# Recurrent layers of a hybrid encoder: three buffers for the mixed inputs, projections in another order, mixing in two groups, and two modulation rounds moved

## What is computed

```python
shift, scale, gate = split(silu(c) @ W_mod + b_mod)
hn = rmsnorm(x) * (1 + scale) + shift
x = x + gate * mixer(hn)
```

```python
xx = 0.5 * (shift_right(h) + shift_left(h)) - h
mu_cols = concat(mu[i] for each column group i)
proj = h @ w_in + xx @ (w_in * mu_cols)      # = (h + mu_i * xx) @ w_in, group by group
r, k, v, g, wl, al = split(proj)
# decay from tanh(wl), rate from al, then the recurrence over time in two directions,
# a norm for each head, times silu(g), times w_out
```

## Time and profile before

| | |
|---|---|
| median of 3 runs | 4082.78 us (4078.05 to 4083.08) |
| the profiled execution | 4076.46 us |
| its span, first to last instruction | 4074.7 us |
| busy PE, VectorE, ScalarE | 84%, 51%, 28% of the span |
| mean granted clock of TensorE | 0.925 |
| layer 0: first BH activation, first gate matmul, L534 | 76.01, 102.64, 251.10 us |
| layer 3: first norm multiply, first gate matmul, L534 | 2764.46, 2791.74, 2929.19 us |

### The profile page before, as it was taken

One profiled execution on the slowest core, in us unless ns is written; L12 is line 12 of the kernel. 1 busy time (PEld: TensorE's weight loads), 2 busy tenths in 40 slices (PEclk: granted clock), 3 DMA queues, 4 the chain that ended last, 5 costly groups with the idle time before them and its releaser, 6 DMA issues. The chain is left out here.

```text
span 4074.7 us, 97171 instructions
## 1 busy us (share of the span) xinstructions
PE 3435.6 (84%) x41792; PEld 2461.1 (60%) x41792; DVE 2096.6 (51%) x4027; ACT 1126.1 (28%) x2792; POOL 0.2 (0%) x4
## 2 busy tenths in 40 slices
PE   4978888888888777989987899487788998889978
PEld 3556766766776644666664555254477667676665
DVE  2254544544454325776773299723455545555542
ACT  2023333332333222333231111112133333333330
POOL 0000000000000000000000000000000000000000
PEclk9988999999999888999998899688899999999989
DMA  3021101111111130010101111021000000000003
GB/s 142 31 80 50 66 26 46 60 33 45 55 50 40 62 108 29 30 43 32 33 36 52 64 52 52 16 89 41 27 14 19 19 12 14 14 19 18 13 20 106
DMA packets 65826, 179.05 MB, mean 44 GB/s; under 512 B 9105, under 2 KB 22545, under 8 KB 65425
## 3 DMA queue, kind: packets, MB, share of 16 engines
q1 hardware_dynamic: 53472, 144.02, 10.5%
q10 hardware_dynamic: 11952, 29.04, 1.9%
HBM read 157.30 MB, written 15.73 MB: 42 GB/s over the span
## 5 line engine op out<-in xcount | busy, mean ns | idle before, releaser
L1632 DVE SCALAR_TENSOR_TENSOR RBF<-bank,ID 128x256 bf16<-128x256 f32 x480 | 192.8, 421 | 409.6 <-PE bank L615 400.7
L954 PE MATMUL bank<-BY,W 128*128 128x384 f32 x1024 | 345.9, 498 | 48.0 <-DVEq L1709 35.2
L813 PE MATMUL bank<-BH,W 128*128 128x384 f32 x1024 | 342.8, 490 | 6.9 <-ACT HZ L1218 6.6
L954 PEld LDWEIGHTS bank<-BY,W 128*128 128x128 f32 x1024 | 196.7, 194 | 181.8 <-DVEq L1709 35.9
L813 PEld LDWEIGHTS bank<-BH,W 128*128 128x128 f32 x1024 | 191.8, 192 | 137.0 <-issue 16.7
L954 PE MATMUL bank<-BX,W 128*128 128x384 f32 x640 | 220.4, 500 | 61.4 <-DVE BX L1955 61.0
L1040 PE MATMUL bank<-BH,W 128*128 128x384 f32 x768 | 250.7, 490 | 15.8 <-DMA W<-in_cf_w_in 15.8
L1678 DVE SCALAR_TENSOR_TENSOR CACC<-CU,CV,CACC 128x798 f32<-128x798 f32 x232 | 224.1, 1041 | 0.0
L735 PE MATMUL bank<-BH,W 128*128 128x384 f32 x512 | 214.3, 549 | 8.9 <-DVE BH L1955 8.9
L1040 PEld LDWEIGHTS bank<-BH,W 128*128 128x128 f32 x768 | 147.2, 192 | 119.8 <-DMA W<-in_cf_w_in 16.9
L954 PEld LDWEIGHTS bank<-BX,W 128*128 128x128 f32 x640 | 121.3, 194 | 160.5 <-issue 67.6
(11 more groups left out here) (273 smaller groups left out, 6378.5 us busy)
## 6 DMA issues: line engine op xcount, KB each, us to landing
W<-in_mod_w SPq DMA_DIRECT2D x96, 512.0 KB, 3.6
W<-in_rw_w_in SPq DMA_DIRECT2D x68, 512.0 KB, 3.9
W<-in_hy_w_in SPq DMA_DIRECT2D x32, 512.0 KB, 6.8
x_scratch<-BX ACTq DMA_DIRECT2D x32, 384.0 KB, 4.2
W<-in_cf_w_in SPq DMA_DIRECT2D x24, 512.0 KB, 3.5
W<-in_rw_w_out SPq DMA_DIRECT2D x16, 512.0 KB, 4.2
W<-in_hy_w_out SPq DMA_DIRECT2D x8, 512.0 KB, 3.8
W<-in_cf_w_out SPq DMA_DIRECT2D x8, 512.0 KB, 4.2
```

The costliest lines, as they stand in the source:

```text
L813: mm = pe.matmul(pj(h), W[:, s, k, :], BH[:, k, tok(h)], start=(k == 0), stop=(k == KT - 1))
L954: mm = pe.matmul(pj(h), lhs(k), rhs(k, h), start=(k == 0), stop=(k == nk - 1))
L1632: v.scalar_tensor_tensor(RBF[:, d, :, :], xout(d), -1.0, bc(ID2[:, 1 if r < NBF else 0, :], GC), ALU.mult, ALU.add).then_inc(ir_ready, 1)
```

## The change

Three areas of memory now hold mixed inputs: BX as before, and BZ1 and BZ2, which lie where the pairs' buffers will be later. MPW gets a place of its own. The ten products are one list, `FRONT`: first tile 32 (wl), then the eight gate tiles, then tile 33 (al). Tile 32 and 33 read BZ1, the gates read BZ2.

The first two mixes are computed in another form: h * (1 - mu) + (mu / 2) * (sum of neighbours). ScalarE writes h * (1 - mu) into BZ1 and BZ2 (16 copies with a scale for each channel); VectorE adds the second term in place (`early_lerp`). The neighbour sum and the first mix are done in two groups of four k, and `norm` goes through both halves of a k before the next k. BD = 0.5 * BD - BH, and the mixes for al, r and k, stand behind the gate instructions of VectorE, four instructions after each gate tile. In layer 0 PE runs the two late modulation rounds before the first product; ScalarE's copies for them stand behind k = 5 of BH and behind the last BZ2 copy. SP loads the rounds' tiles before the ten projection tiles, and the first pair's tiles behind them.

```diff
+FRONT = (32,) + tuple(range(24, 32)) + (33,)
...
+        own("BEHIND", [P, 2 * P + 2 * T + NV_RW + 5])
+        BZ1, BZ2 = own("BZ1", [P, KT, T]), own("BZ2", [P, KT, T])
+        MPW = own("MPW", [P, 4 * P])
...
@@ SP
-                    tiles((l, "gate"), 2, lambda i, s: cols(win, i * 4 + (24 + s)))
-                    tiles((l, "lora"), 1, lambda i, s: cols(win, 32 + s))
                     if with_mods(l):
                         tiles("gates", MOD_REST, lambda i, s: cols(a["mod_w"][l], i * 4 + (MOD_FIRST * 4 + s)), MOD_FIRST)
+                    base = plan[(l, "front")][1]
+                    for t in range(10):
+                        load(t % 4, cols(win, FRONT[t]), free[t % 4] if t < 4 else (pj_full[1], base + t - 3))
+                    for s, t in enumerate((8, 9, 6, 7)):
+                        free[s] = (pj_full[1], base + t + 1)
...
@@ PE
+                    if with_mods(l):
+                        for i in range(MOD_REST):
+                            pe.wait_ge(mod_free, MOD_FIRST + 1)
...
+                            pe.sem_inc(mod_part, 1)
+                            pe.wait_ge(mod_copy, MOD_FIRST + i + 1)
+                            for s in range(4):
+                                o = 8 * i + 2 * s
+                                mm = pe.matmul(IV[:, o:o + 2], MPW[:, s * P:(s + 1) * P], SEL[:, :], start=True, stop=True)
+                            mm.then_inc(mod_sel, 1)
+                    base = plan[(l, "front")][1]
...
+                    for t in range(10):
+                        s, src = t % 4, BZ1 if t in (0, 9) else BZ2
+                        pe.wait_ge(w_ready[s], (plan[(l, "front")][0][s] + t // 4 + 1) * 16)
+                        done(product(base + t, lambda k: W[:, s, k, :], lambda k, h: src[:, k, tok(h)], KT,
+                                     lerped({0: 0, 1: 1, 9: 2}[t]) if t in (0, 1, 9) else None), s)
-                    if with_mods(l):
-                        mod_rounds("gates", MOD_FIRST, MOD_REST)
...
@@ ScalarE, norm of a recurrent layer
+                        for k in range(KT + 1):
+                            for h in range(2 if k < KT else 0):
...
+                            if k:
+                                act.wait_ge(h_ready, n * 2 * KT + 2 * k)
+                                act.activation(BZ1[:, k - 1, :], BH[:, k - 1, :], ACT.Copy, scale=MX[:, 0, k - 1:k]).then_inc(t_ready, 1)
+                            if k == 5 and with_mods(l):
+                                mod_copies(MOD_FIRST)
+                        for k in range(KT):
+                            act.activation(BZ2[:, k, :], BH[:, k, :], ACT.Copy, scale=MX[:, 1, k:k + 1]).then_inc(t_ready, 1)
+                        if with_mods(l):
+                            mod_copies(MOD_FIRST + 1)
...
@@ ScalarE, the ten products
+                    for t in range(10):
+                        for h in range(2):
+                            act.wait_ge(pj_full[h], base + t + 1)
+                            if t == 0:
+                                act.activation(TW[:, 0, tok(h)], pj(h), ACT.Tanh).then_inc(pj_free[h], 1)
+                            elif t == 9:
+                                act.copy(TW[:, 1, tok(h)], pj(h)).then_inc(pj_free[h], 1)
+                            else:
+                                act.wait_ge(pj_free[h], base + t)
+                                act.activation(TT[:, t % 2, tok(h)], pj(h), ACT.Tanh, scale=0.5).then_inc(g_tanh[h], 1)
...
@@ VectorE
+                    for i, m in enumerate((4, 3)):
+                        C.mark(v.tensor_scalar(MX[:, i, :], MU[:, l // 3, m, :], -1.0, 1.0, ALU.mult, ALU.add))
+                        C.link(v.tensor_scalar(MX[:, 2 + i, :], MU[:, l // 3, m, :], 0.5, None, ALU.mult))
...
+                elif l % 3 == 0:
+                    v.wait_ge(r_full, n * 2 + 2)
+                    for k in range(KT):
+                        for h in range(2):
+                            v.tensor_tensor(BD[:, k, tok(h)], BX[:, k, tok(h)], rb[h], ALU.mult).then_inc(xn_ready, 1)
...
+            def early_lerp(dst, rw, i, ks):
+                for k in ks:
+                    v.wait_ge(t_ready, rw * 2 * KT + i * KT + k + 1)
+                    v.scalar_tensor_tensor(dst[:, k, :], BD[:, k, :], MX[:, 2 + i, k:k + 1], dst[:, k, :], ALU.mult, ALU.add).then_inc(lerp_ready, 1)
...
-                    C.link(v.scalar_tensor_tensor(BD[:, :, :], BD[:, :, :], 0.5, BH[:, :, :], ALU.mult, ALU.subtract))
-                    lerp(BX, l, 3)
...
+                    for g in range(2):
+                        ks = slice(4 * g, 4 * g + 4)
+                        v.wait_ge(h_ready, n * 2 * KT + 8 * g + 8)
...
+                        early_lerp(BZ1, rw, 0, range(4 * g, 4 * g + 4))
+                    early_lerp(BZ2, rw, 1, range(KT))
+                    v.wait_ge(lerp_ready, rw * 6 * KT + 2 * KT)
+                    if with_mods(l):
+                        v.wait_ge(mod_sel, MOD_FIRST + MOD_REST)
...
+                    for t in range(1, 9):
                         for h in range(2):
+                            v.wait_ge(g_tanh[h], rw * 8 + t)
+                            v.scalar_tensor_tensor(BY[:, t - 1, tok(h)], TT[:, t % 2, tok(h)], 1.0, pj(h), ALU.add, ALU.mult).then_inc(pj_free[h], 1)
+                        ks = range((t - 1) % 2 * 4, (t - 1) % 2 * 4 + 4)
+                        if t < 3:
+                            for k in ks:
+                                last = C.mark(v.scalar_tensor_tensor(BD[:, k, :], BD[:, k, :], 0.5, BH[:, k, :], ALU.mult, ALU.subtract))
+                        elif t < 5:
...
+                            lerp(BZ1, l, 5, ks)
+                        elif t < 7:
+                            lerp(BX, l, 0, ks)
+                        else:
...
+                            lerp(BH, l, 1, ks)
```

More of the change, by code:

```diff
@@ L107, in __exit__ @@
         c.n = 0
-PER = {"act": {"gate": 0}, "dve": {"mod": 0, "gates": 0, "gate": 0, "pair": 76, "hy": 188, "cf": 34}}
+PER = {"act": {}, "dve": {"mod": 0, "pair": 76, "hy": 188, "cf": 34}}
 def trunk_program(nc, a, out, layers=(0, 1, 2, 3)):
@@ L313, in trunk_program @@
             if l % 3 == 0:
-                phase((l, "gate"), 2, range(4), 8)
-                phase((l, "lora"), 1, range(2), 2)
                 if l == layers[0]:
                     phase("gates", MOD_REST, range(4), 0)
+                plan[(l, "front")] = (tuple(ring), prod)
+                for t in range(10):
+                    ring[t % 4] += 1
+                prod += 10
                 phase((l, "pair"), 8, range(3), 8 * 2)
@@ L1332, in _, with mod_copies @@
             act.sem_inc(ce_ready, 1)
+            def mod_copies(i):
+                act.wait_ge(mod_part, i + 1)
+                act.copy(MPW[:, :], SQB[:, :]).then_inc(mod_copy, 1)
             def mod_rounds(before, rounds):
@@ L1336, in mod_rounds @@
                     act.wait_ge(mod_part, i + 1)
-                    act.copy(MPW, SQB[:, :]).then_inc(mod_copy, 1)
+                    act.copy(MPW[:, :], SQB[:, :]).then_inc(mod_copy, 1)
             def norm(l):
@@ L1357, in norm @@
                         act.wait_ge(x_out, 16 * KT * n)
+                    if l % 3 == 0:
+                        for k in range(KT + 1):
+                            for h in range(2 if k < KT else 0):
+                                act.wait_ge(xn_ready, n * 2 * KT + 2 * k + h + 1)
+                                for t0, t1, st in (((0, HALF, 0),) if h == 0 else ((HALF, LP, 0), (LP, T, 1))):
+                                    ins = act.activation(BH[:, k, t0:t1], BD[:, k, t0:t1], ACT.Identity, scale=GS[:, k, st:st + 1],
+                                                         bias=MOD[:, l * 24 + k, st:st + 1])
+                                ins.then_inc(h_ready, 1)
+                            if k:
[7 more added lines that the diff above has]
+                            mod_copies(MOD_FIRST + 1)
+                        return
                     for h in range(2):
@@ L1369, in _ @@
                     rw = RW[l]
[L1370 to L1378, removed]
-                        for h in range(2):
-                            act.wait_ge(pj_full[h], base + s + 1)
-                            ins = act.activation(TW[:, s, tok(h)], pj(h), ACT.Tanh if s == 0 else ACT.Copy)
-                            ins.then_inc(pj_free[h], 1)
+                    base = plan[(l, "front")][1]
+                    for t in range(10):
+                        for h in range(2):
+                            act.wait_ge(pj_full[h], base + t + 1)
[6 more added lines that the diff above has]
+                                act.activation(TT[:, t % 2, tok(h)], pj(h), ACT.Tanh, scale=0.5).then_inc(g_tanh[h], 1)
                     for h in range(2):
-                        act.wait_ge(pj_free[h], base + 3)
+                        act.wait_ge(pj_free[h], base + 11)
                     act.sem_inc(tw_ready, 1)
-                    if with_mods(l):
```

(20 more changed lines are left out.)

61 lines of the change are left out of this document (29 added, 32 removed).

## The result

| | before | after |
|---|---|---|
| median | 4082.93 us (4078.05 to 4089.84, 4 runs) | 4045.49 us (4042.56 to 4050.05, 4 runs) |
| ratio | | 0.9908 (0.989 to 0.9926) |
| span of the profiled execution | 4074.7 us | 4040.8 us |
| mean granted clock | 0.925 | 0.922 |

The kernel is 37 us faster. The forecast was 4014 us, 69 us faster, and 4045 lies above its range of 4002 to 4032. The stretch that the diff rewrites went as worked out; what stands behind it didn't stay as it was.

The account below looks back on a forecast made before the run. PE, busy 84% of 4074.7 us, gives time back only where it waits or runs at half clock. Layer 3's 32.7 plus layer 0's 36.0 make 68.7 us off 4082.78: 4014, range 4002 to 4032 for 8 in 10.

Parts of the forecast that it names:

- The norm multiply and ScalarE: Layer 3: norm multiply waits for both broadcast halves, 1.3 us lost; ScalarE's new one-pointer copies take 0.83 us each.
- The start of PE and the idle piece: Layer 3: PE starts projections at 2778.9, 12.8 us sooner, then idles 4.1 us between k groups; layer 0 starts at 104.3.
- Without a gap: Nine products after the first follow without PE waiting, 92.9 us, since deferred mixing fits between VectorE's gate instructions.
- W2: Weight loads before the first pair land 6.0 us after PE ends tile 9, no longer hidden, and release the lora matmuls.
- the finish line: Start of the lora matmuls ending the rewritten stretch: forecast 31.7 us sooner in layer 3, 36.0 in layer 0.
- What follows (tanh, decay, scans) is the same code before and after: Behind the lora matmuls' start in both layers: unchanged code, so the change is worth what it moves these two starts.
- the 1.0 of L545: Layer 3's lora matmuls run at full clock, 1.14 us as in layer 0 instead of 2.09: 1.0 us back.
- something behind absorbs part: Rival, 12%: first pair meets a late weight or modulation tile; layer 0 gives back up to half of 36 us: 4032.
- The clock as a rival of its own: Half clock persists in projections; loses from 13 or 14 of 40 half products, all 4220; 4% shared with other waits.
- the gates held by VectorE: Rival: VectorE's work per gate product grows from 4.9 to 14.6 us, losing 68.7; hardly possible, within 4% for slower.

## Why the prediction was wrong

**The norm multiply and ScalarE: right.** The wait for both halves cost 1.3 us, 1.97 us idle instead of 0.67. But I had counted it in layer 3 only; layer 0 has the same wait, and its norm multiply came 1.7 us later (39.60 to 41.28). A pointer-scale copy is 0.92 us long and one follows the other after 0.83, (6.70 - 0.92)/7, the value taken. The Trainium skill, page "ScalarE: Activation LUTs", section "What ACT_TABLE_LOAD costs", gave 0.83 by its formula; the trace agrees.

**The start of PE and the idle piece: right.** Forecast 13.1 us behind the norm multiply and 4.1 us idle, measured 13.24 and 3.98. Layer 0: 104.3 forecast, 104.91 measured, directly behind the selecting matmuls.

**"Without a gap": right.** One line of 312 records; the half product stayed at 5.16 us, and no instruction of the gates was released by the deferred mixing.

**W2: right.** 131.7 us forecast for the finish line, 132.02 measured; in layer 0 it came 34.9 us sooner, 36.0 forecast. L545 took 1.14 us, as taken.

**"What follows (tanh, decay, scans) is the same code before and after": this step failed.** It is the same code at another place. Of the 68.7 us, 34.9 and 31.4 (32.7 less the 1.3 of the wait) and the 1.0 of L545 were there, 67.3 in all, and 33.4 went behind the finish lines: 28.0 in layer 3's pairs, which the three runs with empty instructions show to be the place of VectorE's loop (taken away by 64 of them in the kernel after, made by 16 in the kernel before). The six turns themselves account for 15.5 of the 28. The other 12 go with PE's longer busy time, 14.0 us in six pairs at a granted clock of 0.92 to 0.94 for 0.94 to 0.96; that the stops at the turns bring this about is argued and not shown, for no run took it apart. The 1.3 us of layer 0's pairs and 4.4 us between its end and layer 3's norm multiply are within what executions differ by: the latter piece was between 1482.5 and 1488.2 us in all kernels, which have the same work there. The start of layer 0 varies too: its old finish line, 251.10, came at 246.18, 251.21 and 251.51 in the three kernels of before with empty instructions, so the 34.9 is good to some 5 us.

The rival "something behind absorbs part", with 12 in 100, named the right place and the wrong reason, a late weight or modulation tile, and a bound of 4032 that had nothing to do with the cause. The clock as a rival of its own and the gates held by VectorE did not happen.

The sign of the error could have been found before: in the profile of before, layer 0's turns took 3.20 us and layer 3's 0.70, with nearly the same code. I read neither against the other, and a change that adds 15 instructions ahead of the loop had to raise the question which of the two it would get.

## What to carry to other kernels

When two loops with the same body take different time for each turn, look at the first instruction behind the branch: idle time with no releaser, together with packets on the instruction queue in every turn, says that the body is brought again. Then try the kernel with some tens of empty instructions ahead of the loop before any change is judged, since otherwise a good edit is charged, or a bad one paid, with 20 to 30 us that belong to its position; here the change's 61 to 64 us looked like 37. And "the same code as before" is a claim about work, not about time: a step that costs what follows at nothing should name what else could differ in it.

## What the runs showed of the hardware that I had not expected

- VectorE's loop of 290 instructions: 0.7 us at the turn in one position, 3.2 to 3.4 us in another, with five packets of 8 KB for each turn. The seven pairs from first to last copy, 896.8 us, get 28.0 us longer, 4.0 each.
- The edge is sharp: loop end at the 1983rd instruction good, at the 1986th and 1987th bad. All positions seen fit blocks of 128 instructions with an edge 63 to 65 past a multiple of 128 and three blocks that stay: layer 3's loop ended at 51, 63, 107, 116, 121, 122 and 2 past a multiple (good) and 66 and 67 (bad), layer 0's at 12, 16, 17 and 18 (good) and 84 and 89 (bad). By this about one position in four is bad for a body of 290.
- The convolution layer's loop of 342 instructions fits the same blocks: it ended at 100 and 105 past a multiple where it stood at its turns, and at 28, 32, 33 and 34 where it didn't. It also tells two readings apart. Blocks of 256 instructions of which two stay would fit both pair loops as well, but at 100 and 105 this loop would lie over two of them, and it stood for 3.2 to 3.5 us. That three blocks stay is worked out from these positions; no run took a loop much shorter or longer.
- The same stop costs nothing there: its two turns fell from 3.2 to 3.5 us to 0.8, and the piece of the span that holds them did not get shorter by more than executions differ. What the time hangs on there, no run tried.
- Two profiled executions of one kernel, with the same turns, had 979.2 and 989.6 us for layer 0's pairs, though their times (3986.04 and 3997.37) lie within the spread of the runs. A single profile does not tell 10 us in the pairs.
